# Interleaving the first two projections, moving four weight splits to VectorE, and naming one table set for the roots

## What is computed

```python
def trunk(x, ...):
    for i in range(2):
        h = rmsnorm(x, norm_mix[i])
        if i == 0: m, s = gla_mixer(h, ...)        # gated linear attention, 4 heads
        else:      m, s = shortconv_mixer(h, ...)  # split in three, conv of width 3, gate
        x = x + m
        f, s = conv_ffn(rmsnorm(x, norm_ffn[i]), ...)   # 1024 -> 5632, conv, silu gate, 2816 -> 1024
        x = x + f
    return rmsnorm(x, norm_final), ...

def rmsnorm(x, g):
    return x * rsqrt(mean(x * x, axis=-1) + EPS) * g
```

## Time and profile before

| | before |
|---|---|
| median of 3 runs | 1591.28 us (1588.23 to 1594.64) |
| the profiled execution: its time | 1584.27 us |
| the profiled execution: its span | 1582.5 us |
| TensorE matmul busy | 1536.3 us, 97% |
| VectorE busy | 1123.9 us, 71% |
| ScalarE busy | 458.6 us, 29% |
| GpSimd busy | 516.0 us, 33% |

### The profile page before, as it was taken

How to read it: one execution, slowest core, us unless ns; L and a number is a source line. 1 busy time by engine, 2 the same in 40 slices (tenths; PEclk the granted TensorE clock), 3 DMA queues, 4 the chain that set the end, 5 groups by cost and what they waited for, 6 DMA issues and landing times.

```text
span 1582.5 us, 26037 instructions
## 1 busy us (share of the span) xinstructions
PE 1536.3 (97%) x10292; PEld 1516.2 (96%) x10292; DVE 1123.9 (71%) x1313; ACT 458.6 (29%) x717; POOL 516.0 (33%) x221
## 2 busy tenths in 40 slices
PE   6999999999999999999998999998999999999994
PEld 5999998899999999999998999998999999999994
DVE  6656665854977777877787545557977678777777
ACT  5335555443212212122115111115222121222124
POOL 4422221143233333333233333323333333332331
PEclk8999999999999999999999999999999999999997
DMA  5221115222122222221222222222222222222211
GB/s 210 67 67 54 54 54 218 105 71 69 65 81 71 77 69 77 80 68 64 80 80 67 78 69 81 78 67 69 67 68 80 68 78 80 72 62 78 81 38 67
DMA packets 34873, 123.76 MB, mean 78 GB/s; under 512 B 3920, under 2 KB 6864, under 8 KB 33648
## 3 DMA queue, kind: packets, MB, share of 16 engines
q1 hardware_dynamic: 31872, 108.37, 21.3%
q10 hardware_dynamic: 2928, 14.35, 2.4%
HBM read 114.48 MB, written 8.22 MB: 78 GB/s over the span
## 4 chain that ended last, share of the span: by engine, by line
PE 91%; DVE 6%; DVEq 1%; ACT 1%; issue 1%; DMA 0%; POOL 0%; SPq 0%; ACTq 0%
PE ps L401 62%; PE ps L417 20%; PE ps L484 2%; PE ps L584 2%; DVE sq L728 1%; DVE xl L712 1%; PE ps L691 1%; DVE x L761 1%; PE ps L536 1%; PE ps L608 1%; DVEq L726 1%; PE ps L498 1%; PE ps L429 0%; DMA x<-x_t 0%; DVE x L1115 0%
## 5 line engine op out<-in xcount | busy, mean ns | idle before, releaser
L345 POOL TENSOR_TENSOR wl<-raw,wh 128x1024 fp32r<-128x1024 f32 x195 | 489.3, 2515 | 962.1 <-ACT wh L1177 962.1
L401 PE MATMUL ps<-xh,wh 128*128 128x328 f32 (+5 forms) x2176 | 506.5, 314 | 15.2 <-DVE xl L712 14.9
L401 PE MATMUL ps<-xl,wh 128*128 128x328 f32 (+5 forms) x2176 | 503.2, 313 | 0.0
L401 PE MATMUL ps<-xh,wl 128*128 128x328 f32 (+5 forms) x2176 | 502.7, 313 | 0.0
L401 PEld LDWEIGHTS ps<-xh,wh 128*128 128x128 f32 x2176 | 389.5, 190 | 18.3 <-issue 9.4
L401 PEld LDWEIGHTS ps<-xl,wh 128*128 128x128 f32 x2176 | 390.0, 190 | 0.0
L401 PEld LDWEIGHTS ps<-xh,wl 128*128 128x128 f32 x2176 | 389.5, 190 | 0.0
L1177 ACT ACTIVATE wh<-raw 128x1024 fp32r<-128x1024 f32 x196 | 204.3, 1055 | 299.6 <-PE ps L401 276.5
L761 DVE TENSOR_TENSOR x<-ps,x 128x644 f32<-128x644 f32 (+2 forms) x208 | 164.9, 822 | 95.1 <-PE ps L417 69.4
L965 DVE SCALAR_TENSOR_TENSOR y<-zp,par,y 128x660 f32<-128x660 f32 (+1 forms) x192 | 185.6, 967 | 26.9 <-issue 22.1
L417 PE MATMUL ps<-gl,wh 128*128 128x322 f32 (+1 forms) x800 | 184.5, 312 | 0.0
(11 more groups left out here) (154 smaller groups left out, 1185.3 us busy)
## 6 DMA issues: line engine op xcount, KB each, us to landing
raw<-w_units SPq DMA_DIRECT2D x196, 512.0 KB, 3.5
s<-states ACTq DMA_DIRECT2D x4, 1024.0 KB, 5.7
state_sample<-snew ACTq DMA_DIRECT2D x4, 1024.0 KB, 4.1
x<-x_t SPq DMA_DIRECT2D x8, 328.0 KB, 6.1
x<-x_t ACTq DMA_DIRECT2D x1, 2624.0 KB, 12.7
y_t<-x SPq DMA_DIRECT2D x6, 320.0 KB, 2.4
ffn_last<-zl ACTq DMA_DIRECT2D x2, 396.0 KB, 2.4
zc<-ffn_cache ACTq DMA_DIRECT2D x1, 704.0 KB, 4.2
```

The lines of the kernel that those rows point to most:

```text
L345: pool.tensor_tensor(wl[:, j, :, :], raw[:, j, :, :], wh[:, j, :, :].bitcast(F32), ALU.subtract).then_inc(sem["lo_done"], 1)
L401: mm = pe.matmul(ps[:, p, c:c + z - a], w[:, ring, k, :], v[:, k, a:z], start=(k == 0 and w is wh and v is hi), stop=(k == KT - 1 and w is ...
```

## The change

It does four things.

1. **The start.** The norm's sum gets PSUM slot 0, ahead of `k` and `q` of head 0. TensorE runs units 0 and 1 together (`project_first_two`): for each k-step it waits for `xl` of tile k, does the six matmuls of unit 0 and the six of unit 1. The sum of norm 0 follows after both. Unit 2's projection gives `units_used` a count of 2, since the interleaved ones give none. SyncE loads unit 1 directly after x tile 0, and ScalarE does `high(1)` directly after `xh` of tile 0.
2. **Squares and low parts at the start.** ScalarE makes all eight squares of norm 0. VectorE makes the low parts of units 0 and 1; the second stands between `xl` of tile 0 and `xl` of tile 1. GpSimd begins with unit 2.
3. **The mid norms.** At the end of `update_x` for n = 2 and 3, VectorE makes the low parts of two units (100 and 101, 132 and 133). GpSimd's list has a wait in their place.
4. **Table sets.** `root` and the last stage load the set `natural_log_exp_and_others` by name in place of the tiny Ln, and a load of the set `natural_log` is put ahead of the Ln of the gate.

```diff
@@ -65,7 +65,9 @@
 assert FIRST_Z[0] + STEP == FIRST_MIX == FIRST_Z[1]
 META = 16
 assert FIRST_Z[1] + STEP == META
-POOL_SQ = [0, 2, 4]
+MIX_START = 2 * HEADS + 16 + KT + ZT + FT
+NORM_UNITS = {2: MIX_START + 2, 3: MIX_START + 3 * KT + KT + 2}
+LOG_EXP = "natural_log_exp_and_others"
 POOL_OUT = 3
 MIX_G = 4
...
@@ -116,7 +118,7 @@
 def plan_slots():
     s = SlotPlan()
-    s.straight(("k", 0), ("q", 0), ("norm", 0), "gate_down")
+    s.straight(("norm", 0), ("k", 0), ("q", 0), "gate_down")
     s.straight(("k", 1), *[("gate_up", h) for h in range(HEADS)])
     s.straight(("q", 1), *[(kind, h) for h in range(2, HEADS) for kind in "kq"])
     for h in range(HEADS):
...
@@ -318,7 +320,7 @@
         sp.dma_start(par[:, 0:C_FFN], par_in[:, 0:C_FFN]).then_inc(sem["par_in"], 16)
         for k in range(KT):
             sp.dma_start(x[:, k, :], x_in[:, k, :]).then_inc(x_in_s[k], 16)
-            if k == KT - 3:
+            if k == 0:
                 sp.dma_start(raw[:, 1, :, :], w_in[1]).then_inc(landed[1], 16)
         sp.dma_start(par[:, C_FFN:], par_in[:, C_FFN:]).then_inc(sem["more_par_in"], 16)
         for j in (2, 3):
...
@@ -345,11 +347,8 @@
             pool.tensor_tensor(wl[:, j, :, :], raw[:, j, :, :], wh[:, j, :, :].bitcast(F32),
                                ALU.subtract).then_inc(sem["lo_done"], 1)
-        for n, m in enumerate(POOL_SQ):
-            pool.wait_ge(x_in_s[m], 16)
-            pool.tensor_tensor(sq0[:, m, :], x[:, m, :], x[:, m, :], ALU.mult).then_inc(sem["pool_sq_done"], 1)
-        pool.wait_ge(sem["lo_done"], 1)
-        for j in range(1, RING):
+        pool.wait_ge(sem["lo_done"], 2)
+        for j in range(2, RING):
             low(j, j + 1)
         before_out = (2 * HEADS + 16) // RING
         with pool.Fori(0, before_out) as i:
...
@@ -359,9 +358,17 @@
             pool.wait_ge(sem["oh_done"], k + 1)
             pool.tensor_tensor(ol[:, k, :], qk[:, k, :], oh[:, k, :].bitcast(F32),
                                ALU.subtract).then_inc(sem["o_done"], 1)
-        with pool.Fori(0, N_UNITS // RING - 1 - before_out) as i:
-            for j in range(RING):
-                low(j, RING * i + (RING * (1 + before_out) + j + 1))
+        done = RING * (1 + before_out)
+        for u in (NORM_UNITS[2], NORM_UNITS[3], N_UNITS):
+            assert done % RING == u % RING == 0
+            with pool.Fori(0, (u - done) // RING) as i:
+                for j in range(RING):
+                    low(j, RING * i + (done + j + 1))
+            if u < N_UNITS:
+                pool.wait_ge(sem["lo_done"], u + 2)
+                low(2, u + 3)
+                low(3, u + 4)
+                done = u + RING
         for c in range(2):
             pool.wait_ge(sem["gained"], POOL_OUT * (c + 1))
...
@@ -439,12 +446,31 @@
             return lambda k: norm_sum(n) if k == KT // 2 else None
+        def project_first_two():
+            places = [open_slot(("k", 0)), open_slot(("q", 0))]
+            for k in range(KT):
+                pe.wait_ge(sem["xs_lo"], k + 1)
+                for unit, p in enumerate(places):
+                    if k == 0:
+                        weights(unit + 1)
+                    for w, v in ((wh, xh), (wh, xl), (wl, xh)):
+                        for c, a in ((0, 0), (BANK, HALF)):
+                            mm = pe.matmul(ps[:, p, c:c + HALF], w[:, unit, k, :], v[:, k, a:a + HALF],
+                                           start=(k == 0 and w is wh and v is xh),
+                                           stop=(k == KT - 1 and w is wl))
+                    if k == KT - 1:
+                        mm.then_inc(filled[p], 1)
         pe.wait_ge(sem["consts"], 1)
+        project_first_two()
+        norm_sum(0)
+        n_unit = 2
         for h in range(HEADS):
             for j, kind in enumerate("kq"):
-                project((kind, h), xh, xl, n_unit + 1, n_unit % RING, release=1 if n_unit else 0,
-                        before=(x_ready(0), norm_amid(0))[j] if h == 0 else None)
-                n_unit += 1
+                if h:
+                    project((kind, h), xh, xl, n_unit + 1, n_unit % RING, release=2 if n_unit == 2 else 1)
+                    n_unit += 1
                 if (kind, h) == ("k", 1):
                     copied("gate_down")
...
@@ -717,11 +743,7 @@
             if m == 0:
                 return
-            if n:
-                dve.wait_ge(sem["sq_done"], KT * n - len(POOL_SQ) + m + 1)
-            else:
-                dve.wait_ge(sem["pool_sq_done"], sum(t <= m for t in POOL_SQ))
-                dve.wait_ge(sem["sq_done"], sum(t <= m and t not in POOL_SQ for t in range(KT)))
+            dve.wait_ge(sem["sq_done"], KT * n + m + 1)
             if m > 1:
                 dve.drain()
             total, src = (sq0 if n == 0 else sq)[:, 0, :], (sq0 if n == 0 else sq)[:, m, :]
...
@@ -759,6 +781,13 @@
             tile, product = from_token(first, x[:, m, :], p)
             dve.tensor_tensor(tile, product, tile, ALU.add).then_inc(freed[p], 1)
+        def low(u):
+            j = u % RING
+            dve.wait_ge(sem["hi_done"], u + 1)
+            dve.tensor_tensor(wl[:, j, :, :], raw[:, j, :, :], wh[:, j, :, :].bitcast(F32),
+                              ALU.subtract).then_inc(sem["lo_done"], 1)
         def update_x(steps, first, n):
...
@@ -772,19 +801,20 @@
             split_low(n, KT - 1)
             for m in [KT - 1] if n == 1 else range(KT):
                 add_square(n, m)
-        dve.wait_ge(sem["hi_done"], 1)
-        dve.tensor_tensor(wl[:, 0, :, :], raw[:, 0, :, :], wh[:, 0, :, :].bitcast(F32),
-                          ALU.subtract).then_inc(sem["lo_done"], 1)
+            if n in NORM_UNITS:
+                dve.wait_ge(sem["lo_done"], NORM_UNITS[n])
+                low(NORM_UNITS[n])
+                low(NORM_UNITS[n] + 1)
+        low(0)
         dve.wait_ge(sem["par_in"], 16)
         for m in range(KT):
             split_low(0, m)
-            if 2 <= m < KT - 2:
-                add_square(0, m - 2)
-        for m in range(KT - 4, KT):
-            add_square(0, m)
+            if m == 0:
+                low(1)
+            if m > 1:
+                add_square(0, m - 1)
+        add_square(0, KT - 1)
         dve.wait_ge(sem["gla_in"], 48)
         dve.tensor_copy(wgd[:, :, 0:16], wgd_raw[:, :, :])
         dve.drain()
...
@@ -1137,7 +1167,7 @@
         def root(step, r, d, c=None):
-            act.activation(tiny[:, :], ones[:, 0:1], ACT.Ln)
+            act.preload_act_table_set(LOG_EXP)
             p = take(step)
             out, src = (two(r), slot(p)) if c is None else (r, bank(p, c))
             act.activation(out, src, ACT.Ln, scale=1.0 / d,
...
@@ -1184,9 +1214,9 @@
         for m in range(KT):
             act.wait_ge(x_in_s[m], 16)
             split_high(0, m)
-            if m == KT - 2:
+            if m == 0:
                 high(1)
-            if m and m - 1 not in POOL_SQ:
+            else:
                 square(0, m - 1)
         act.dma_start(reset[:, :], reset_in).then_inc(sem["gla_in"], 16)
         square(0, KT - 1)
...
@@ -1206,6 +1236,7 @@
         act.drain()
         act.activation(soft[:, :, :], soft[:, :, :], ACT.Exp, scale=-1.0)
         act.drain()
+        act.preload_act_table_set("natural_log")
         act.activation(soft[:, :, :], soft[:, :, :], ACT.Ln, bias=1.0).then_inc(sem["soft_done"], 1)
         for u in range(6, 2 * HEADS + RING):
             high(u)
...
```

More of the change, by code:

```diff
@@ L260, in build @@
     names = ["par_in", "more_par_in", "gla_in", "wgd_done", "hi_done", "lo_done", "units_used", "consts",
-             "xs_hi", "xs_lo", "sq_done", "pool_sq_done", "sum_done", "log_done", "root_done", "soft_done", "mask_in", "d_done", "e_done",
+             "xs_hi", "xs_lo", "sq_done", "sum_done", "log_done", "root_done", "soft_done", "mask_in", "d_done", "e_done",
              "lev_done", "r_silu", "dec_done", "chain_stored", "osq_done", "osum_done", "o_done", "o_scaled", "oh_done", "x_back",
@@ L1094, in add_last_square @@
         def add_last_square(c, m):
-            dve.wait_ge(sem["sq_done"], KT * (4 + c) - len(POOL_SQ) + m + 1)
+            dve.wait_ge(sem["sq_done"], KT * (4 + c) + m + 1)
             if m > 1:
```

## The result

| | before | changed |
|---|---|---|
| median (range) of 4 runs each | 1590.36 us (1588.23 to 1594.64) | 1563.6 us (1561.81 to 1566.72) |
| ratio, 95% interval | | 0.9834 (0.9808 to 0.9860) |
| profiled execution: time, span | 1584.27, 1582.5 | 1561.81, 1560.0 |
| TensorE busy | 97% | 98% |
| ScalarE, GpSimd busy us | 458.6, 516.0 | 447.5, 494.5 |

The forecast was 1567.9, with 1562.5 to 1578.0 as its range. The two profiled executions differ by 22.5 us, where the sum said 23.4; the medians of the first runs differ by 26.8. The changed kernel's profiled execution is the fastest of its four.

The account below looks back on a forecast made before the run. TensorE, busy 97%, was taken to bound the kernel, improvable only through its pauses and half clock. Start 10.3, mid norms 13.1 and table sets 0 sum to 23.4 us: 1591.28 - 23.4 = 1567.9 us, range 1562.5 to 1578.

Parts of the forecast that it names:

- The start: Units 0 and 1 and norm 0: unit 2 would start at 31.9 instead of 42.19 us, saving 10.3 us.
- The mid norms: Norms 2 and 3: TensorE's waits for the sums go entirely, saving 6.6 and 6.5 us, together 13.1 us.
- VectorE's low parts cost nothing on the path: Behind the sums of norms 2 and 3: two low parts of 1.23 us on VectorE don't hold up the root.
- The table sets: Roots and last norm: the named load costs 1.28 us where 1.28 is saved, so 0 was taken.
- The step from profile to median: Whole kernel: the median stands 7.0 us above the profiled execution, and this was assumed to stay.
- The start's upper end of 11.5: Units 0 and 1 and norm 0: the most the start could save was put at 11.5 us.
- The upper end of 1578: Whole kernel: slowest time in the range, said to hold rival 1, one kept mid norm and 3.4 us of spread.
- rival 1: Start: unit 1 lands late and tiles queue behind its high part; saving 7 instead of 10.3, 1571 us; chance 0.12.
- 2: Start: the clock stays low while units 0 and 1 interleave; unit 2 at 45.5, total 1581.5 us; chance 0.04.
- 3: Norms 2 and 3: waits stay because additions are late for another reason; 1574.5 or 1581 us; chance 0.09.
- 4: Start and mid norms: other traffic, such as loads, stretches VectorE, not GpSimd; slower, 1611 us; chance 0.03.
- 5: Last norm: the named set doesn't serve both functions, a load before Exp remains; 1569.2 us; chance within the forecast's 0.72.

Follow-up runs that it names:

- e2: The kernel before with only the low parts of units 100, 101, 132 and 133 moved from GpSimd to VectorE; ratio to before 0.9902, span 1573.8 us.
- e7: The changed kernel plus three useless GpSimd subtractions on an unused tile at norms 2 and 3; span 1580.7 us.
- e3: The kernel before with only the named table sets; ratio to before 0.9986, span 1583.0 us.
- e12: The changed kernel with unit 1 loaded behind x tile 5 again, its high part still right behind tile 0; unit 2 started 5.1 us later.
- e8: The changed kernel plus eight useless GpSimd memsets on an unused tile at norms 2 and 3; span 1569.8 us.
- e4: The changed kernel with GpSimd's first low parts held until VectorE finishes the start, and the last norm's repeated loads left out; 1565.25 us, ratio to before 0.9858.
- e5: The changed kernel with TensorE's old order of units 0 and 1 and the old PSUM slots; unit 2 started at 36.66 us.
- e1: The changed kernel with only its start, mid norms and table sets as before the change; ratio to before 0.9951, span 1582.1 us.
- e6: The changed kernel with squares of tiles 0, 2, 4 and unit 1's low part back on GpSimd; unit 2 started at 36.27 us.

## Why the prediction was right, by its steps

- **The start: 9.7 us against 10.3.** Every link was there: `high(1)` at 7.83 (7.6), 1.38 per tile on ScalarE (1.39), the last split at 19.59 (19.3), half clock until 13.8, no wait for a tile, root 0 off the path. The first tile came 0.3 us later, but both units ended at 25.48, in the middle of the 25.0 to 26.0 that I had worked out. What was late is the sum, which waited 0.82 us for the last two additions, stretched from 1.7 to 5.8 us. I had allowed up to 0.7 for that on top of 31.1 to 32.1; the 31.9 that I took is 0.3 above the middle of that range, without a term of its own.
- **The mid norms: 13.1 against 13.1.** e2 and e7 show the cause as well: taken away in one, brought back in the other.
- **VectorE's low parts cost nothing on the path**, as said. The root of norm 2 was refined at 854.1, and TensorE did not wait. GpSimd's unit 102 ran from 849.15 to 851.55 and stretched one multiplication by 0.1 us only; I had said 2.0 for one or two. It fell beside an idle VectorE and then beside an operation that reads PSUM, which kept its 0.90.
- **The table sets: 0 against 0.** A repeated load is executed; I had left that open and taken the right side. e3 shows that this part alone would have had 0.5 us, at norm 0. It vanishes behind the interleaving.
- **The step from profile to median** was the weak one. I let 7.0 us stand between them; in the first runs it was 1.8. The forecast was 4.3 us too high: 5.2 us by this step, less the 0.9 us of gain that the sum had too much. With more executions it is 5.4 before and 5.0 after. The step was right in kind, and the first median was low, if anything.
- **Where luck helped.** In both profiled executions the heads' stretch ran at full clock, which it did in 5 of the 14 traces here. And 42.19 belongs to an execution in which all three of GpSimd's low parts fell on splits; against one like e2's the same new start would have gained 7.1. The agreement of 22.5 with 23.4 is closer than one pair of executions can promise.
- **Slips in the range.** The start's upper end of 11.5 doesn't follow from the steps: 42.19 - 31.1 is 11.1. The upper end of 1578 holds rival 1 and one kept mid norm; with the 3.4 of the spread it would be 1581. And rival 1 was priced too low: I took 3.3 us, and e12 lost 5.1. The measured 1563.6 lies near the lower end, where neither matters.
- **Rivals.** 1 is real as a mechanism (e12) and was avoided by landings in the order of issue. 2 did not occur at the start. A relative of it, which I hadn't seen, occurs in the heads' stretch. 3 fell with the waits at norms 2 and 3, 4 by e2, e7 and e8. 5 fell in the trace: no load stands ahead of Exp.

## What to carry to other kernels

When an elementwise operation of VectorE takes three times its usual time, look at what GpSimd does in that very stretch before giving GpSimd more work. Moving a short operation onto the "busier" engine can free it, if it takes away a collision at the place where TensorE waits. A pause of TensorE costs its length and then the half clock behind it, so price both: pauses of 4.9 us cost 6.6 here. And a span of one execution should be compared mark by mark: a stretch that nobody touched moved by 9 us here, and a start that nobody touched by 2.6.

## What the runs showed of the hardware that I had not expected

- The heads' stretch, with the same 432 matmuls and TensorE busy 98 to 100% of it, ran at a granted clock of 1.00 in the profiled executions of before, of the changed kernel, e3, e4 and e5, and partly at 1.2 GHz in those of e1, e2, e6 to e12 (66.7 against 68 to 76 us). A wait ahead of it doesn't decide it: in e4 TensorE waited 1.5 us for VectorE's new states there and kept the full clock, in e1 it waited for nothing there and lost 9.4 us. What decides it is open; I made no run that changes TensorE's work in that stretch.
- GpSimd's memsets (8.47 us of them) left VectorE's additions at their speed, and three subtractions of 7.33 us in all cost them 4.6 us.
- The same program can start 2.6 us earlier or later by which of VectorE's operations GpSimd's low parts fall on (before and e2).
- A load of a table set that is already in place is executed all the same, for 1.28 us.
